# Attention of a two-layer mixer with keys instead of queries on the partitions

## The chip, the core and the metric

The kernel runs on one core of a Trainium2 chip, in one launch. The metric is the device time of a whole execution in microseconds (us), as the median of several runs. PE is TensorE, DVE is VectorE, ACT is ScalarE, POOL is GpSimd and SP is SyncE.

## What is computed

Two layers act on a sequence of 512 positions of width 1024. Each layer normalizes, projects, runs four branches (short convolution, sparse attention, retention, pooled means), gates and merges them, and ends with a gated feed-forward part. The change touches the attention branch:

```python
s_c = einsum('bsgjd,bngd->bgjsn', q, k_c)            # 31 compressed keys
p_c = masked_softmax(s_c, mask_c) * mask_c
o_cmp = einsum('bgjsn,bngd->bsgjd', p_c, v_c)
...
# o_slc, o_win: causal softmax attention over all 512 keys
# (all 8 blocks are among the 16 chosen, the window is 512 wide)
o = g[..., 0:1] * o_cmp + g[..., 1:2] * o_slc + g[..., 2:3] * o_win
```

There are eight heads in two key groups of four, each 64 wide. The selected and the window branch have keys and values of their own, so there are 16 causal attentions of 512 by 512 a layer.

## The kernel before

All activations lie transposed, features on partitions and 512 positions along the free axis. Every dense projection is a tile of 128 features by 512 positions in one of two PSUM banks (`acc`). It is made in full precision from F32R products: for each chunk of 128 inputs, `product` (L1107 to L1109) issues weights' high part by activations' high part, high by low, and low by high. Below, a product is one such 128x512 matmul.

Weights stream in groups of eight chunks through a ring of three buffers. SP loads `w_raw`, ACT rounds it to `w_hi` (L431), POOL subtracts to `w_lo` in two halves (L415), and each starts on a buffer when PE has left it. DVE empties each tile (`take`, L650) and PE may use a bank again when that is done. A layer runs stage A (12 groups: keys, values, queries, gates), stage B (32 groups: inputs of the other branches), the merge, the output projection and the feed-forward part.

The small work of the branches is spread over stage B. A group's four quarters, six products each, are the **slots**, 128 in all. The table `SIDE` names for each slot the steps that stand behind its products, and all engines walk through the same table in the same order, so the order on every queue is fixed by hand. Engines meet at counting semaphores.

Attention takes slots 4 to 71. Queries are on the partitions. A unit is one branch, one block of 128 queries and one head; two heads, one of each key group, go together, on the upper and lower 64 rows of PE's array. `scores` (L1266) makes a row of up to 512 scores. DVE adds the causal mask and takes the row's maximum in one instruction (L823). ACT takes the exponential with the maximum as its bias and the row's sum on the side (L513), and scales by gate over sum (L519). PE turns the probabilities in 128x128 pieces (`turn`, L1274), DVE copies them out of PSUM (L842), and `values` (L1292) multiplies. The compressed scores are eight small matmuls for each block of queries (L1253), masked, scaled and turned likewise; their values join the same output bank.

Retention follows with four heads (`RET_SLOT`). `ret_scores` (L1316) is multiplied by a decay table on DVE (L872) and feeds `ret_values` (L1326). The table comes by a DMA on ACT's queue (L498). The rotation of retention's queries and keys needs their halves exchanged, by two DMAs on ACT's queue (`rotate_partners`, L459, L460), and three DVE operations (L690 to L694).

## Time and profile before

| | before |
|---|---|
| median of 3 runs | 2152.51 us (2152.16 to 2152.82) |
| profiled execution | 2152.31 us |
| its span | 2150.5 us |
| PE, DVE, ACT, POOL busy | 97%, 57%, 31%, 43% |

Busy time of PE counts overlapping records once, and the records' ends are modelled; the distance between two starts tells what a matmul costs. Positions are us from the span's start. Line numbers are those of the kernel before.

### The profile page before, as it was taken

How to read it: one execution, taken by the hardware profiler on the slowest of the kernel's cores; microseconds unless marked ns; L12 is line 12 of the kernel's file. 1: busy time of each engine (PE TensorE's matmuls, PEld its weight loads, DVE VectorE, ACT ScalarE, POOL GpSimd, SP SyncE). 2: the span in 40 equal slices, each digit the busy share in tenths (PEclk: the TensorE clock that was granted, in tenths of full speed). 3: DMA queues.
4: the chain of work that ended last, by engine and by line, in shares of the span. 5: the costliest groups of instructions: out<-in, count | busy, mean ns of one | idle time of the engine just before them, and what ended most of it. 6: DMA issues, size and time to landing. Idle time of an engine off the chain costs nothing.

```text
span 2150.5 us, 32302 instructions
## 1 busy us (share of the span) xinstructions
PE 2086.4 (97%) x9834; PEld 1643.1 (76%) x9834; DVE 1227.3 (57%) x1856; ACT 659.8 (31%) x961; POOL 920.8 (43%) x676
## 2 busy tenths in 40 slices
PE   7999989999999999999999999999999999999997
PEld 5766667788888788888877666668888887888885
DVE  8656766622235888872157568565223278888513
ACT  3244423333332222222223445223233322222222
POOL 3422223444444555545534222234444454555552
PEclk9999999999999999999999999999999999999998
DMA  5311122222222222223232111222322232222332
GB/s 188 103 55 50 50 64 89 85 93 96 98 98 98 88 98 98 98 90 109 98 122 93 50 40 50 77 86 88 102 94 96 98 98 89 97 98 98 101 107 98
DMA packets 57131, 194.90 MB, mean 91 GB/s; under 512 B 6864, under 2 KB 7248, under 8 KB 56912
## 3 DMA queue, kind: packets, MB, share of 16 engines
q1 hardware_dynamic: 52272, 186.14, 26.1%
q10 hardware_dynamic: 4768, 7.61, 1.4%
q8 instruction: 50, 0.82, 0.2%
q14 instruction: 41, 0.34, 0.1%
HBM read 186.64 MB, written 2.10 MB: 88 GB/s over the span
## 4 chain that ended last, share of the span: by engine, by line
PE 91%; DVE 6%; issue 2%; ACT 0%; DMA 0%; DVEq 0%; ACTq 0%; SPq 0%
PE acc L1107 27%; PE acc L1109 27%; PE acc L1108 27%; PE o L1292 2%; PE s L1266 2%; PE t L1274 2%; PE o L1326 1%; PE s L1253 1%; PE s L1316 1%; PE s L1183 0%; PE t L1303 0%; DVE ssq L639 0%; DVE xg_lo L618 0%; PE s L1342 0%; DVE y_lo L900 0%
## 5 line engine op out<-in xcount | busy, mean ns | idle before, releaser
L415 POOL TENSOR_TENSOR w_lo<-w_raw,w_hi 128x512 fp32r<-128x512 f32 x672 | 920.6, 1390 | 1202.1 <-ACT w_hi L431 1190.4
L1107 PE MATMUL acc<-xg_hi,w_hi 128*128 128x512 f32 x1904 | 780.1, 410 | 18.4 <-DVE xg_lo L618 11.5
L1109 PE MATMUL acc<-xg_hi,w_lo 128*128 128x512 f32 x1904 | 748.9, 393 | 0.0
L1108 PE MATMUL acc<-xg_lo,w_hi 128*128 128x512 f32 x1904 | 748.0, 393 | 0.0
L431 ACT ACTIVATE w_hi<-w_raw 128x1024 fp32r<-128x1024 f32 x336 | 355.1, 1057 | 902.0 <-PE acc L1109 837.8
L1107 PEld LDWEIGHTS acc<-xg_hi,w_hi 128*128 128x128 f32 x1904 | 360.8, 190 | 127.3 <-issue 38.8
L1109 PEld LDWEIGHTS acc<-xg_hi,w_lo 128*128 128x128 f32 x1904 | 361.0, 190 | 77.8
L1108 PEld LDWEIGHTS acc<-xg_lo,w_hi 128*128 128x128 f32 x1904 | 361.7, 190 | 76.4 <-issue 6.9
L987 DVE TENSOR_TENSOR work<-acc,rstd 128x512 f32<-128x512 f32 x64 | 44.1, 690 | 256.1 <-PE acc L1109 256.1
L1107 PE MATMUL acc<-act_hi,w_hi 128*128 128x512 f32 x352 | 136.9, 389 | 0.0
L1108 PE MATMUL acc<-act_lo,w_hi 128*128 128x512 f32 x352 | 136.9, 389 | 0.0
L1109 PE MATMUL acc<-act_hi,w_lo 128*128 128x512 f32 x352 | 136.9, 389 | 0.0
L1081 DVE SCALAR_TENSOR_TENSOR x<-acc,x 128x512 f32 x16 | 11.1, 693 | 177.5 <-PE acc L1109 177.5
L993 DVE SCALAR_TENSOR_TENSOR work<-work,acc 128x512 f32<-128x512 f32 x64 | 44.0, 687 | 103.1 <-PE acc L1109 103.1
L1107 PE MATMUL acc<-y_hi,w_hi 128*128 128x512 f32 x256 | 99.6, 389 | 0.0
L1108 PE MATMUL acc<-y_lo,w_hi 128*128 128x512 f32 x256 | 99.6, 389 | 0.0
L1109 PE MATMUL acc<-y_hi,w_lo 128*128 128x512 f32 x256 | 99.6, 389 | 0.0
L566 ACT ACTIVATE work<-work 128x512 f32<-128x512 f32 x44 | 27.8, 632 | 186.4 <-DVE work L1036 186.4
L1108 PEld LDWEIGHTS acc<-act_lo,w_hi 128*128 128x128 f32 x352 | 66.1, 188 | 13.8
L1107 PEld LDWEIGHTS acc<-act_hi,w_hi 128*128 128x128 f32 x352 | 66.1, 188 | 13.7
L1109 PEld LDWEIGHTS acc<-act_hi,w_lo 128*128 128x128 f32 x352 | 66.1, 188 | 13.7
L842 DVE COPY pT<-t 128x128 f32<-128x128 f32 (+3 forms) x128 | 56.8, 486 | 28.3 <-PE t L1274 27.4
(190 smaller groups left out, 2231.1 us busy)
## 6 DMA issues: line engine op xcount, KB each, us to landing
w_raw<-weights_dram SPq DMA_DIRECT2D x339, 512.0 KB, 3.3
x<-xT_dram SPq DMA_DIRECT2D x8, 256.0 KB, 6.1
rot<-rq ACTq DMA_DIRECT2D x16, 128.0 KB
rot<-rk ACTq DMA_DIRECT2D x16, 128.0 KB
dec<-decay_dram ACTq DMA_DIRECT2D x8, 256.0 KB, 3.6
out_dram<-x SPq DMA_DIRECT2D x8, 256.0 KB, 2.2
con<-consts_dram SPq DMA_DIRECT2D x1, 1598.0 KB, 10.8
w1k<-w_dram SPq DMA_DIRECT2D x2, 512.0 KB, 9.3
```

Of the source, the lines that this page charges most:

```text
L415: nc.gpsimd.tensor_tensor(w_lo[:, k, part], w_raw[:, k, part], w_hi[:, k, part].bitcast(F32), ALU.subtract).then_inc(lo_ready, 1)
L431: nc.scalar.activation(w_hi[:, slot, :], w_raw[:, slot, :], ACT.Copy).then_inc(hi_ready, 1)
L566: nc.scalar.activation(work[:, 2, :], work[:, 1, :], ACT.Tanh, scale=0.5).then_inc(silu_ready, 1)
L842: t_end(ve.tensor_copy(pT[:, u % 2, 0:w], t_of(e)[:, 0:w]), e)
L987: ve.tensor_tensor(work[:, n, :], acc[n % 2][:, :], rstd[:, :], ALU.mult).then_inc(acc_free, 1)
L993: ve.scalar_tensor_tensor(out=work[:, n, :], in0=work[:, n, :], scalar=1.0, in1=acc[n % 2][:, :], op0=ALU.add, op1=ALU.mult).then_inc(acc_ ...
L1107: mm(tile, w_h, right_hi, start=first, stop=False)
L1108: mm(tile, w_h, right_lo, start=False, stop=False)
L1109: return mm(tile, w_l, right_hi, start=False, stop=last)
L1266: mm(b[:, 0:w], qT[r, h % 4, qi * P:(qi + 1) * P], kT[r, br, 0:w], start=True, stop=True).then_inc(s_done, 1)
L1274: ins = nc.tensor.transpose(b[:, k * P:(k + 1) * P], pr_of(u)[:, k * P:(k + 1) * P], ident)
L1292: ins = mm(o_bank[qi % 2][d, j * P:(j + 1) * P], v[:, d], p[:, half, :], start=(br == 0 and k == 0), stop=(br == 1 and k == qi + 1))
```

## The change

Keys now lie on the partitions and the probabilities come out in the orientation that the values need, so nothing is turned. The maximum runs along partitions then, so it is found ahead.

- **Maxima.** In slots 4 to 43, 40 quarters, PE makes all scores once more with queries on partitions, from F32R copies, into two banks a visit (`max`, 32 visits; `cmp_max`, 4). DVE writes minus the maximum into `table`. In slot 45 PE turns the table into rows, `shift`.
- **Pairs.** From slot 49 on, eight pairs (a branch and one head of each key group) take two slots each. A visit `scores` makes two blocks of keys for both heads: a first matmul with a repeated column of the identity adds the shift, a second the scores. ACT takes exponentials straight from PSUM, POOL zeroes what lies in the future (`affine_select`), and `values` multiplies. DVE adds the four blocks (`sums`), and PE sums that over partitions (`sum`) with selectors, 16 equal rows a head.
- **Factors.** `share`: DVE takes the reciprocal of a branch's sums and multiplies by the gates; ACT's queue spreads each row over 64 partitions with eight DMAs; `merge` multiplies and adds. There are three, for compressed, selected and window branch.
- **Homes and banks.** The two branches' outputs have buffers of their own. The scores ring has four banks in place of two and two for turns. Head 0 of retention moves from slot 68 to 71, and its decay table to the group of slot 68.

```diff
+PAIRS = 2 * BC
+VISITS = ((0, 3), (1, 2))
+MAX_SLOT = 4
+MAXES = [("max", _br, _qi, _j) for _br in range(2) for _qi in range(QT) for _j in range(BC)]
+for _n, _e in enumerate(MAXES):
+    SIDE[MAX_SLOT + 5 * _n // 4].append(_e)
+for _qi in range(QT):
+    SIDE[MAX_SLOT + 10 * _qi + 9].append(("cmp_max", _qi))
+TURN_SLOT = MAX_SLOT + 41
+SIDE[TURN_SLOT].append(("max_turn",))
+SIDE[TURN_SLOT + 1].append(("cmp_scores",))
+SIDE[TURN_SLOT + 3] += [("cmp_sum",), ("cmp_values",)]
+SIDE[TURN_SLOT + 4].append(("share", 0))
+PAIR_SLOT = [TURN_SLOT + 4 + 2 * _p for _p in range(PAIRS)]
+for _p in range(PAIRS):
+    SIDE[PAIR_SLOT[_p]].append(("scores", _p, 0))
+    SIDE[PAIR_SLOT[_p] + 1].append(("scores", _p, 1))
+for _p in range(PAIRS):
+    SIDE[PAIR_SLOT[_p] + 1].append(("values", _p, 0))
+    SIDE[PAIR_SLOT[_p] + 2] += [("values", _p, 1), ("sums", _p)]
+    SIDE[PAIR_SLOT[_p] + 3].append(("sum", _p))
+for _b in range(3):
+    if _b:
+        SIDE[PAIR_SLOT[BC * _b - 1] + 4].append(("share", _b))
+    for _j in range(BC):
+        _s = PAIR_SLOT[BC * _b - 1] + 8 if _b else TURN_SLOT + 9
+        SIDE[_s + _j // 2].append(("merge", _b, _j))
+ATTN_END = PAIR_SLOT[-1] + 4
...
+            def causal_part(L, p, v):
+                pool.wait_ge(con_ready, 16)
+                for k in VISITS[v]:
+                    s_freed(pool, L, ("scores", p, v, k, KV_GROUPS - 1))
+                    alone(pool)
+                    own = p_of(p, k)[:, :, 0:P]
+                    ins = nc.gpsimd.affine_select(own, own, [[0, KV_GROUPS], [1, P]], ALU.is_ge, zero, base=0, channel_multiplier=-1)
+                ins.then_inc(p_ready, 1)
...
+                        if B_TILES[b - 1] == ("rq", 1):
+                            act.wait_ge(v_made, v_count(L, ("merge", 2, 1)))
                         rotate_partners(L, B_TILES[b - 1])
...
+                        if b == max(14 + 4 * h, 17 + h):
+                            if h < 2:
+                                act.wait_ge(pv_done, pv_count(L, ("sum", PAIRS - 1)))
+                            else:
+                                s_freed(act, L, ("ret_scores", h - 2, QT - 1))
                             act.dma_start(dec[:, h % 2, :], decay[h, :, :]).then_inc(dec_ready[h % 2], 16)
...
+                            elif e[0] == "cmp_values":
+                                for j in range(BC):
+                                    act.wait_ge(s_done, s_use(L, (*e, j)))
+                                    free_s(nc.scalar.activation(o_all[:, j, :], s_of((*e, j))[:, :], ACT.Copy), (*e, j))
+                            elif e[0] == "scores":
+                                p, v = e[1], e[2]
+                                if v == 0:
+                                    if p < 2:
+                                        act.wait_ge(pv_done, pv_count(L, ("cmp_sum",)))
+                                        act.wait_ge(s_done, s_use(L, ("cmp_values", BC - 1)))
+                                    else:
+                                        act.wait_ge(pv_done, pv_count(L, ("sum", p - 2)))
+                                if p:
+                                    act.wait_ge(v_made, v_count(L, ("sums", p - 1)))
+                                    act.wait_ge(pv_done, pv_count(L, ("values", p - 1, 1 if v else 0)))
+                                for k in VISITS[v]:
+                                    for g in range(KV_GROUPS):
+                                        use = (*e, k, g)
+                                        act.wait_ge(s_done, s_use(L, use))
+                                        free_s(nc.scalar.activation(p_of(p, k)[:, g, 0:S - k * P], s_of(use)[:, 0:S - k * P], ACT.Exp,
+                                                                    scale=DH ** -0.5), use)
...
+                            elif e[0] == "share":
+                                b_ = e[1]
                                 act.wait_ge(v_made, v_count(L, e))
-                                nc.scalar.activation(cmp_p[:, :, :], cmp_p[:, :, :], ACT.Exp,
-                                                     scale=DH ** -0.5).then_inc(a_made, 1)
-                            elif e[0] == "scores":
-                                u = e[1]
-                                act.wait_ge(s_free, 1 + s_use(L, e) + 1)
-                                nc.scalar.activation(pr_of(u), pr_of(u), ACT.Exp, bias=nmax[:, u % 2:u % 2 + 1], scale=-1.0,
-                                                     accum_out=den[:, u % 4:u % 4 + 1]).then_inc(a_made, 1)
-                            elif e[0] == "scale":
-
-                                act.wait_ge(v_made, v_count(L, e))
-                                for u in (e[1], e[1] + 1):
-                                    nc.scalar.activation(pr_of(u), pr_of(u), ACT.Copy, scale=scl[:, u % 4:u % 4 + 1]).then_inc(a_made, 1)
+                                for j in range(BC):
+                                    if b_:
+                                        act.wait_ge(v_made, v_count(L, ("merge", b_ - 1, j)))
+                                    for g in range(KV_GROUPS):
+                                        row = recip[64 * g + 16 * j + b_:64 * g + 16 * j + b_ + 1, :]
+                                        act.dma_start(shared[64 * g:64 * g + 64, j, :],
+                                                      bass.AP(row.tensor, row.offset, [list(row.ap[0]), [0, DH], [1, S]])).then_inc(share_here[j], 16)
...
+                def max_(e):
+                    br, qi, j = e[1:]
+                    w = (qi + 1) * P
+                    s_wait((*e, KV_GROUPS - 1))
+                    for g in range(KV_GROUPS):
+                        s = s_of((*e, g))[:, 0:w]
+                        at_ = 64 * g + BC * br + j
+                        alone(dve)
+                        s_end(ve.tensor_tensor_reduce(s, s, C("causal", S)[:, S - w:S], -1.0, 3e38, ALU.add, ALU.min,
+                                                      table[:, qi, at_:at_ + 1]), (*e, g))
...
+                def sums(e):
+                    p = e[1]
+                    dve.wait_ge(p_ready, p_ready_count(L, ("scores", p, 1)))
+                    dve.wait_ge(pv_done, pv_count(L, ("values", p, 0)))
+                    for k in (1, 2, 3):
+                        all_ = p_of(p, 0)[:, :, k * P:S]
+                        ins = ve.tensor_tensor(all_, all_, p_of(p, k), ALU.add)
+                        if k < 3:
+                            then(ins)
+                    v_end(ins, e)
+                def share(e):
+                    b = e[1]
+                    dve.wait_ge(pv_done, pv_count(L, ("sum", BC * b - 1) if b else ("cmp_sum",)))
+                    ve.reciprocal(recip[:, :], o_of(("den", b))[:, :]).then_inc(o_free[1], 1)
+                    o_freed(dve, L, ("den", b))
+                    v_end(ve.tensor_tensor(recip[:, :], recip[:, :], gates[:, :], ALU.mult), e)
...
+                    o_freed(dve, L, ("pair", BC * (b - 1) + j))
+                    part = part_of(b, j)
+                    then(ve.tensor_tensor(part, part, shared[:, j, :], ALU.mult))
+                    v_end(ve.tensor_tensor(all_, all_, part, ALU.add), e, wait=(b == 2))
+                    if b == 2:
+                        split_y(1, j, all_)
...
+                def max_(e):
+                    br, qi, j = e[1:]
+                    w = (qi + 1) * P
+                    pe.wait_ge(a_made, a_count(L, f"q_r{j}"))
+                    banks = s_begin(*[(*e, g) for g in range(KV_GROUPS)])
+                    last_wait()
+                    for g, b in enumerate(banks):
+                        r = rows_of(g)
+                        ins = mm(b[:, 0:w], q_r[r, j, qi * P:(qi + 1) * P], k_r[r, br, 0:w], start=True, stop=True)
+                        ins.then_inc(s_done, 1)
...
+                    banks = s_begin(*uses)
+                    pe.wait_ge(const_made, L + 1)
                     last_wait()
-                    mm(b[:, 0:w], qT[r, h % 4, qi * P:(qi + 1) * P], kT[r, br, 0:w], start=True, stop=True).then_inc(s_done, 1)
-
-                def turn(e):
-                    u = e[1]
-                    pe.wait_ge(a_made, a_count(L, ("scale", u)))
-                    b = t_begin(e)
+                    at_ = BC * br + j
+                    four = [(k, rows_of(g), g, banks[uses.index((*e, k, g))]) for k in VISITS[v] for g in range(KV_GROUPS)]
+                    for k, r, g, b in four:
+                        mm(b[:, 0:S - k * P], spread(ident_r[r, 64 * g + at_:], [[0, P]]), shift[r, k * P:S], start=True, stop=False)
+                    for k, r, g, b in four:
+                        mm(b[:, 0:S - k * P], kT[r, br, k * P:(k + 1) * P], qT[r, j, k * P:S],
+                           start=False, stop=True).then_inc(s_done, 1)
...
+                    own = ones_at[:, 16 - 16 * (j % 2):48 - 16 * (j % 2)]
+                    for g in range(KV_GROUPS):
+                        c = 64 * g + 32 * (j // 2)
+                        ins = mm(den[c:c + 32, :], own, p_of(p, 0)[:, g, :], start=(j % 2 == 0), stop=(j % 2 == 1), skip_group_check=True)
+                    ins.then_inc(pv_done, 1)
```

The queue of ACT in the pairs. Before, for two scores steps of 256 keys (`pr_odd`, `pr` are score rows):

```order
L431 ACTIVATE w_hi<-w_raw 128x1024 [waits raw_ready0]
L512 REGISTER_ALU
L513 ACTIVATE pr,small<-pr,small 128x256 [waits s_free]
L512 REGISTER_ALU
L513 ACTIVATE pr,small<-pr,small 128x256 [waits s_free]
L517 REGISTER_ALU
L519 ACTIVATE pr<-pr,small 128x256 [waits v_made]
```

Of the change, where the pairs open (`o_all` takes the compressed values, `shared` the spread factors, `p_` the probabilities of key blocks):

```order
L646 ACTIVATE o_all<-s 128x512 [waits s_done]
L676 REGISTER_ALU
L682 DMA shared<-recip 64x1x512 [waits v_made]
L682 DMA shared<-recip 64x1x512 x7
L651 ISA
L661 REGISTER_ALU [waits s_done,pv_done]
L662 ACTIVATE p_zero_104<-s 128x512 [waits s_done]
L661 REGISTER_ALU
L662 ACTIVATE p_zero_104<-s 128x512 [waits s_done]
```

Eight DMAs now stand between the emptying of the compressed values and the first exponentials.

ACT's queue before the decay table `dec` of retention head 0, before:

```order
L519 ACTIVATE pr_odd<-pr_odd,small 128x512 [waits v_made]
L519 ACTIVATE pr_odd<-pr_odd,small 128x512
L429 REGISTER_ALU
L431 ACTIVATE w_hi<-w_raw 128x1024 [waits raw_ready1,halves]
L498 DMA dec<-decay_dram 128x512
```

Of the change:

```order
L682 DMA shared<-recip 64x1x512
L530 REGISTER_ALU
L532 ACTIVATE w_hi<-w_raw 128x1024 [waits raw_ready1,halves]
L616 REGISTER_ALU
L556 REGISTER_ALU [waits v_made]
L558 REGISTER_ALU [waits acc_free]
L560 DMA rot<-rq 64x512 [waits v_made]
L561 DMA rot<-rq 64x512
L623 REGISTER_ALU
L626 DMA dec<-decay_dram 128x512 [waits pv_done]
```

The rotary DMAs with their wait, and the last of the share DMAs, now stand ahead of it.

DVE at the first retention scores, before:

```order
L650 TENSOR_TENSOR rq<-acc,rstd 128x512 [waits halves]
L651 REGISTER_ALU
L655 REGISTER_ALU [waits acc_free]
L868 ISA [waits s_done]
L872 TENSOR_TENSOR pr<-s,dec 128x512 [waits dec_ready0]
L665 REGISTER_ALU
L841 REGISTER_ALU [waits t_done]
L842 COPY pT<-t 128x512 [waits pv_done]
```

Of the change (`o_early`, `o_third` hold window outputs):

```order
L1032 TENSOR_TENSOR o_all<-o_all,o_early 128x512 [waits chain]
...
L1072 CAST y_hi_56<-o_all 128x512 [waits v_made]
...
L1073 TENSOR_TENSOR y_lo_60<-o_all,y_hi_56 128x512 [waits chain]
...
L1045 TENSOR_TENSOR pr<-s,dec 128x512 [waits dec_ready0]
...
L1031 TENSOR_TENSOR o_third<-o_third,shared 128x512 [waits o_free0]
...
L1032 TENSOR_TENSOR o_all<-o_all,o_third 128x512 [waits chain]
...
L1072 CAST y_hi_56<-o_all 128x512 [waits v_made]
...
L1073 TENSOR_TENSOR y_lo_60<-o_all,y_hi_56 128x512 [waits chain]
...
L1045 TENSOR_TENSOR pr<-s,dec 128x384 [waits s_done]
```

Merges now stand before and between the two retention scores.

## Rows read from the trace of the kernel before

**Rows 1.** The page, parts 1, 4 and 5.

```profile
PE 2086.4 (97%) x9834; PEld 1643.1 (76%) x9834; DVE 1227.3 (57%) x1856; ACT 659.8 (31%) x961; POOL 920.8 (43%) x676
...
PE 91%; DVE 6%; issue 2%; ACT 0%; DMA 0%; DVEq 0%; ACTq 0%; SPq 0%
...
L415 POOL TENSOR_TENSOR w_lo<-w_raw,w_hi 128x512 fp32r<-128x512 f32 x672 | 920.6, 1390 | 1202.1 <-ACT w_hi L431 1190.4
...
L431 ACT ACTIVATE w_hi<-w_raw 128x1024 fp32r<-128x1024 f32 x336 | 355.1, 1057 | 902.0 <-PE acc L1109 837.8
```

**Rows 2.** The timeline of PE: start and duration in us, line, operation, tiles.

```profile
1000.19 0.39 PE L1107 MATMUL acc<-act_hi,w_hi 128*128 128x512 f32 x1
...
1005.63 0.39 PE L1107 MATMUL acc<-act_hi,w_hi 128*128 128x512 f32 x1
```

**Rows 3.** Busy time by stretch of line L1107 alone, second layer.

```profile
1154.40:1354.00 199.60, 61.24 (x136) 25.78 (x135) 0.98 0.17 55
```

**Rows 4.** The timeline of PE around a scores and a values step.

```profile
201.29 0.40 PE L1109 MATMUL acc<-xg_hi,w_lo 128*128 128x512 f32 x1
201.62 0.92 PE L1266 MATMUL s<-kT,qT 64*128 64x384 f32 x4
...
202.80 0.39 PE L1108 MATMUL acc<-xg_lo,w_hi 128*128 128x512 f32 x1
...
203.73 0.40 PE L1109 MATMUL acc<-xg_hi,w_lo 128*128 128x512 f32 x1
204.06 0.88 PE L1292 MATMUL o<-pT,v_nat 128*64 128x128 f32 x12
...
205.23 0.87 PE L1274 MATMUL t<-con,pr 128*128 128x128 f32 x6
...
206.17 0.39 PE L1108 MATMUL acc<-xg_lo,w_hi 128*128 128x512 f32 x1
```

**Rows 5.** The timeline of PE around a compressed-scores step.

```profile
229.56 0.40 PE L1109 MATMUL acc<-xg_hi,w_lo 128*128 128x512 f32 x1
229.89 1.87 PE L1253 MATMUL s<-kc,qT 64*128 64x31 f32 x13
...
233.99 0.40 PE L1108 MATMUL acc<-xg_lo,w_hi 128*128 128x512 f32 x1
```

**Rows 6.** The timeline of ACT, two neighbours of 512 columns.

```profile
1357.70 0.60 ACT L527 ACTIVATE pT<-o 128x512 f32<-128x512 f32 x1 [4.57 <-issue]
1358.19 0.59 ACT L528 ACTIVATE pT<-o 128x512 f32<-128x512 f32 x1
```

**Rows 7.** Groups of DVE instructions by form: busy us, mean ns, idle before.

```profile
L1091 DVE RECIPROCAL rstd<-rstd 128x512 f32<-128x512 f32 x1 | 3.4, 3353 | 2.7 <-ACT rstd L585 2.7
...
L937 DVE TENSOR_TENSOR y_lo<-sc,y_hi 128x512 fp32r<-128x512 f32 x8 | 9.5, 1193 | 0.1
...
L933 DVE TENSOR_TENSOR sc<-sc 128x512 f32<-128x512 f32 x8 | 5.5, 693 | 0.3
```

**Rows 8.** The timeline of ACT, DMA issues of the rotary partners.

```profile
49.62 0.63 ACTq L453 DMA_DIRECT2D rot<-kT  x1
50.28 0.63 ACTq L452 DMA_DIRECT2D rot<-kT  x1
```

**Rows 9.** Line L459: duration ns min/median/max of the issues.

```profile
L459 ACTq DMA_DIRECT2D rot<-rk x8: 468/468/482, 109.7 to 1427.3; - x8
```

**Rows 10.** The tile of the decay table.

```profile
DMA to landing us min/median/max: 2.6/3.6/4.8
```

**Rows 11.** PE before and at retention head 1, then that stretch's busy time.

```profile
1368.51 0.40 PE L1109 MATMUL acc<-xg_hi,w_lo 128*128 128x512 f32 x1
1372.39 2.07 PE L1316 MATMUL s<-rq,rk 128*128 128x512 f32 x2 [3.49 <-DVE rk L694]
...
1371.60:1378.30 6.70, 5.91 (x10) 3.47 (x11) 3.29 (x6) 0.00 (x0) 0.00 (x0) 0.50 0.23 78
```

**Rows 12.** PE's waits: us in total, times, longest us.

```profile
PE s L1316 <- DVE rk L694: 14.7, 6, 3.5
```

630 lines of the change are left out of this document (364 added, 266 removed).

## The prediction

> **What bounds the kernel now.** I read the page first, then the PE timeline in steady state and around the side steps, then the forms of DVE and ACT work, then the waits. TensorE is busy 97% of the span and holds 91% of the chain that ended last [rows 1]. A busy record says little here, because the records overlap: two records of the same line, 24 products apart, start 5.44 us apart, 0.2267 us per product [rows 2]. The program's 7920 products (3 for each of 2640 chunks) at that pitch are 1795 us of the 2150.5, so the rest of the span is side steps, waits and a slow clock. The kernel is bound by TensorE's queue: each side step is paid in full, and another engine costs something where PE waits for it.
>
> The changed stretch is slots 4 to 71 of stage B. In the second layer it runs from 1154.4 to 1354.0, 199.6 us, with 136 products of each of three lines [rows 3]: 408 products, 92.5 us. The other 107.1 us hold head 0 of the retention (2560 columns of full-array f32 at four passes, 2560/512 x 4 x 0.2267 = 4.5 us), its turn (about 0.5) and attention: **102 us a layer**, its waits included.
>
> **Unit prices on PE.** The scores step at 201.62 stands between products at 201.29 and 202.80 [rows 4]: 1.51 us, less two pitches, is 1.06. It holds a pair of 384-column f32 matmuls on the two row halves. One of them at four passes is 384/512 x 4 x 0.2267 = 0.68, so the second is free and entering and leaving the half-array costs 0.4. The values step at 204.06, from 203.73 to 206.17, costs 2.44 - 0.45 = 1.99: three pairs of 128 columns on column halves (0.68), the compressed pair, six turns at 0.11, and about 0.3 of switching. A compressed-scores step, between products at 229.56 and 233.99, costs 3.98 with a 512-column scores pair of 1.3 in it: 2.7 for matmuls of 31 columns [rows 5].
>
> **The change on PE, per layer.** F32R passes are 0.2267 per 512 columns, f32 four times that; each step pays 0.4 for switching, a step behind another about 0.2.
> - Maxima: 32 F32R pairs of 128 to 512 columns. The pairs cost 0.13 to 0.23 (short ones bounded by weight loads), 5.3 together, with 32 x 0.4: 18.
> - Compressed maxima, 4 x 0.9: 3.6. Mask turn, table turn and gate matmul: 1.8.
> - Scores, 16 visits: main products 8 x 1280 columns x 4 passes = 18.1, shift products 8 x 0.57 = 4.5, switching 6.4: 29.
> - Values: 18.1 + 16 x 0.2 = 21.3. Sums: 8 x (0.91 + 0.2) = 8.9.
> - Compressed scores (16 matmuls on 8 tiles), their sum and values: all tiles together, in rounds of 512/512 x 4 x 0.2267 = 0.9, two rounds, one and one with their switching, 2.3 + 1.2 + 1.3 = 4.8. Two tiles at a time, which is all that the row shows [rows 4], 7.7 + 1.2 + 4.0 = 12.9. I take 4.8, since there the second tile costs nothing visible, and keep 12.9 for the range.
>
> Sum: 87.4, plus 0.7 in stage A for eight small value products instead of two. That is 102 - 88 = **14 us a layer gained**, mostly from 160 probability turns, the compressed-scores steps and 32 f32 scores that become F32R.
>
> **The change in waits, per layer.** Three places queue long work ahead of what PE needs.
>
> *Opening of the pairs (slots 48 to 50).* Let T be the end of the compressed sum on PE. ACT empties four banks first; ACTIVATEs of 512 columns start 0.49 apart [rows 6], so scores (0,0) starts near T+3.2 instead of T+2.6: 0.6 of wait. DVE takes a reciprocal of 512 columns, 3.35 us, and a product of 0.7 [rows 7], done at T+4.3. ACT then issues eight DMAs. Two neighbouring issues are 0.66 apart and each holds the ACT queue for 0.63 [rows 8]; eight take 5.3 us, to T+9.6. Only behind them stand the exponentials of (0,0), 1.4 us. PE has finished scores (0,0) and slot 50's products at T+6.5 and needs their banks: it waits until T+11, **4.5 us**. The shortest issue that the trace shows is 0.47 [rows 9], which would make 3.8 of the 5.3.
>
> *Middle (slot 59).* The same eight DMAs stand before the exponentials of (5,1). Counted from the first finished pair of scores (4,1) at X: exponentials end X+1.4, POOL's selects X+2.1 (256 elements, taken at half of the 1.39 of a 512-element w_lo half [rows 1]; 0.1 to 1.4), the three adds X+4.2, reciprocal and product X+8.5, DMAs X+13.9, w_hi 1.06 [rows 1] and one more issue X+15.4, exponentials X+16.8. PE arrives at X+14: **2.8 us**.
>
> *End (slots 66 to 73).* Before, head 0 found its decay table long loaded. Now its ACT queue reads: eight share DMAs, w_hi, a wait for merge (2,1), two rotary DMAs, then the decay DMA. DVE comes to the sums late, since the last two merges of the first branch and a mean stand before it: 1.6 us for PE, and 0.8 before the reciprocal. With T now the end of the last sum: reciprocal and product T+5.1, the last mean part and a take (about 3.8) T+8.9, merge (2,0) with four operations T+11.6, two operations of merge (2,1) while POOL makes w_lo. Such SBUF-to-SBUF operations range from 0.69 to 1.2 [rows 7]; with 1.2 each T+14.2. Rotary DMAs T+15.5, the decay landing 3.6 later [rows 10] T+19.1, DVE's product T+19.9. PE stands at its first retention value from T+9.7: **10.2 us**. Then merges (2,2) and (2,3), eight operations of 0.69, precede DVE's second retention score: another **4.2 us**.
>
> The table turn in slot 45 waits for DVE's last maxima (two of 0.77 a step, with a convolution among them): 1.3. I add 1.0 for the other 13 visits, whose exponentials (1.4) are covered by 1.4 of products and 1.3 of values. New waits: 0.6 + 4.5 + 2.8 + 1.6 + 10.2 + 4.2 + 1.3 + 1.0 = **26 us a layer**.
>
> **Clock.** Before 1372.39 PE waited 3.49 us, and from 1371.6 to 1378.3 its granted clock was 0.50, the 1.2 GHz level [rows 11]. At half clock 6.7 us of work take what 3.4 would. Three long waits should bring this about up to four times a layer; two dips at the old compressed-scores steps may go. I take **+4**, range 0 to 8.
>
> Net per layer: -14 + 26 + 4 = +16, **+32 us** for two. The profiled execution took 2152.3 around a span of 2150.5, and the median of the runs is 2152.5, so either base gives **2184 us**.
>
> **A rule beside the row.** The scores step [rows 4] shows two tiles at a time and nothing about eight. The Trainium skill (TensorEngine Tiling (Array Packing), Key Properties) says that tiles work independently and may load and multiply in parallel. By that rule the compressed steps cost 4.8; by the pairing alone, 12.9, and the total would be 2200. No row here has more than two tiles at work.
>
> **Rivals.**
> 1. *Faster.* PE's saving is real and the waits shrink: ACT's issues are short, merges run uncontended, exponentials slip into the gaps. Only the decay chain stays, about 5 a layer: 2 x (-14 + 5) = -18, 2134. For it: before, PE lost only 14.7 us to its largest group of waits [rows 12], so its queue is well fed. Against it: the order of the ACT queue and 0.66 per issue. It decides if new waits and clock stay below 14 a layer.
> 2. *DVE bounds the pairs.* The adds of probabilities and merges read two SBUF tensors while POOL works more. If all run at 1.7 times, as y_lo's 1193 against 693 [rows 7], two slots hold 3.6 of sums, 5.3 of convolution, 2.9 of merges and 0.4 of takes, 12.2 us against PE's 10; over five pairs 11 us a layer: 2206. The Trainium skill (GPSIMD Engine Reference, Specifications) names this contention for DVE instructions with two SBUF inputs, and the spread in rows 7 agrees. Against it: POOL is busy only part of a group, and not every pair has convolution and merges.
> 3. *Tiles go two at a time*, for the want of more than two in any row: 2184 + 2 x 8.1 = 2200.
>
> **How the numbers follow.** Forecast 0.50, range of its own 2160 to 2208 (issues 0.47 or 0.66, contention, clock 0 to 8). Rival 1: 0.22. Rival 2: 0.18. Rival 3: 0.10. The 80% range reaches down to rival 1's 2134, since below the forecast it holds most of the chance, and to 2212, above rival 2. About 0.2% (4.3 us) is what a measurement of this kernel tells from no change; only rival 1's weak end lands there. Faster 0.20, same 0.05, slower 0.75.
>
> **What would show it.** In the changed profile PE waits of about 4.5 us at the second scores visit, released by ACT's exponentials; about 10 us at the first retention value, released by DVE's product with the decay table, and 4 at the next; a granted clock of 0.5 just after. Right on PE: max steps of about 0.55, no L1274-like turns. I am wrong if the exponentials start before the share DMAs end, if the retention values start on time, or if the stretch from the first maxima to the first retention score, waits left out, is not some 14 us a layer shorter.

## The result and the profile after

The changed kernel takes **2246.89 us** (median of 4 runs, 2244.48 to 2252.45), the kernel before on the same chip 2152.66: a ratio of 1.0438, 95% interval 1.0424 to 1.0453. The forecast was 2184, at most 2212. The direction is right; of 94 us of loss it had 32.

The page of the changed kernel, its parts 1, 3, 4 and 5, beside [rows 1]:

```profile
PE 2070.0 (92%) x9334; PEld 1601.1 (71%) x9334; DVE 1226.3 (55%) x1682; ACT 587.2 (26%) x739; POOL 953.6 (43%) x744
...
q10 hardware_dynamic: 8608, 13.90, 5.4%
...
PE 82%; DVE 9%; ACTq 5%; issue 3%; ACT 1%; DMA 1%; DVEq 0%; SPq 0%
PE acc L1280 25%; PE acc L1282 25%; PE acc L1281 25%; ACTq L682 4%; PE s L1516 1%; PE o L1531 1%; PE s L1438 1%; DVE recip L1015 1%; PE o L1569 1%; DVE y_lo L1073 1%; PE s L1514 1%; PE s L1559 1%; DMA dec<-decay_dram 1%; DVE p_zero L1006 0%; PE o L1546 0%
```

TensorE has less work and is idle more. New in the chain is ACT's DMA queue with 5%, nearly all of it line 682, the share DMAs. PE's waits (us in total, times, longest), whose largest group was 14.7 before [rows 12]:

```profile
PE o L1569 <- DVE pr L1045: 48.7, 8, 22.0
PE s L1514 <- ACT p_two L662: 30.1, 2, 16.6
PE s L1514 <- ACT p_three L662: 27.9, 2, 14.2
PE s L1559 <- DVE rk L853: 15.0, 6, 3.3
...
PE s L1461 <- DVE table L989: 1.5, 2, 0.8
```

These are the three places of the forecast: the opening (14.2, forecast 4.5), the middle (16.6, forecast 2.8) and the end (22.0, forecast 10.2). ACT's timeline at the opening shows why, beside [rows 8]:

```profile
189.46 2.06 ACT L646 ACTIVATE o_all<-s 128x512 f32<-128x512 f32 x4 [1.55 <-PE s L1499]
192.52 14.94 ACTq L682 DMA_DIRECT2D shared<-recip  x8
207.71 1.08 ACT L662 ACTIVATE p_zero<-s 128x512 f32<-128x512 f32 x2 [16.18 <-issue]
```

Eight issues hold ACT for 14.94 us, not for 5.3. The tile of the spread factors gives one issue (ns, minimum, median, maximum) and its landing:

```profile
L682 ACTq DMA_DIRECT2D shared<-recip x48: 476/1868/4254, 192.5 to 1426.5; - x48
...
DMA to landing us min/median/max: 6.2/7.9/10.1
```

At the end the slow transfers are paid for more than once, first on ACT's timeline:

```profile
310.91 15.03 ACTq L682 DMA_DIRECT2D shared<-recip  x8
...
326.34 1.41 ACTq L560 DMA_DIRECT2D rot<-rq  x1
327.77 2.68 ACTq L561 DMA_DIRECT2D rot<-rq  x1
330.56 0.91 ACTq L626 DMA_DIRECT2D dec<-decay_dram  x1
```

and then on DVE's, where the first merge waits for a landing and the decay product for the table:

```profile
320.28 0.69 DVE L1031 TENSOR_TENSOR o_early<-o_early,shared 128x512 f32<-128x512 f32 x1 [6.93 <-DMA shared<-recip]
...
324.25 0.69 DVE L1031 TENSOR_TENSOR o_early<-o_early,shared 128x512 f32<-128x512 f32 x1 [1.36 <-DMA shared<-recip]
...
336.20 0.69 DVE L1045 TENSOR_TENSOR pr<-s,dec 128x512 f32<-128x512 f32 x1 [9.34 <-DMA dec<-decay_dram]
...
343.07 0.56 DVE L1045 TENSOR_TENSOR pr<-s,dec 128x384 f32<-128x384 f32 x1
```

These operations of DVE themselves run at 0.69, uncontended. Of all share products (`o_all`, `o_slc` and the like from `shared`) the median is 0.69 and the longest 0.99.

PE's own prices are as forecast. Its timeline around a maxima step of 256 columns, and around the compressed scores with their 8 shift and 8 score matmuls, each of which leaves two records:

```profile
115.39 0.39 PE L1282 MATMUL acc<-xg_hi,w_lo 128*128 128x512 f32 x1
115.71 0.39 PE L1438 MATMUL s<-k_r,q_r 64*128 64x256 f32 x2
...
116.36 0.39 PE L1281 MATMUL acc<-xg_lo,w_hi 128*128 128x512 f32 x1
...
182.13 0.40 PE L1282 MATMUL acc<-xg_hi,w_lo 128*128 128x512 f32 x1
182.46 1.09 PE L1473 MATMUL s<-shift,con 64*32 64x512 f32 x16
183.34 1.06 PE L1477 MATMUL s<-qT,kc 64*32 64x512 f32 x16
...
184.67 0.39 PE L1281 MATMUL acc<-xg_lo,w_hi 128*128 128x512 f32 x1
```

Less two pitches [rows 2], the maxima step costs 116.36 - 115.39 - 0.45 = 0.52 (over the four widths 0.47 to 0.64, forecast 0.55), and the compressed scores 184.67 - 182.13 - 0.45 = 2.09 (forecast 2.3).

### The profile page after: what moved, and what is told of

It is laid out like the page before. It is cut to its first block, busy times and chain, and to the rows that moved or that the text cites. A ratio compares the mean times of both kernels' runs of the same rounds, so it can differ in the third digit from the quotient of the medians.

```text
span 2242.7 us, 30172 instructions
## 1 busy us (share of the span) xinstructions
PE 2070.0 (92%) x9334; PEld 1601.1 (71%) x9334; DVE 1226.3 (55%) x1682; ACT 587.2 (26%) x739; POOL 953.6 (43%) x744
## 4 chain that ended last, share of the span: by engine, by line
PE 82%; DVE 9%; ACTq 5%; issue 3%; ACT 1%; DMA 1%; DVEq 0%; SPq 0%
PE acc L1280 25%; PE acc L1282 25%; PE acc L1281 25%; ACTq L682 4%; PE s L1516 1%; PE o L1531 1%; PE s L1438 1%; DVE recip L1015 1%; PE o L1569 1%; DVE y_lo L1073 1%; PE s L1514 1%; PE s L1559 1%; DMA dec<-decay_dram 1%; DVE p_zero L1006 0%; PE o L1546 0%
## 5 line engine op out<-in xcount | busy, mean ns | idle before, releaser
L1006 DVE TENSOR_TENSOR p_zero<-p_zero,p_one 128x768 f32<-128x768 f32 x16 | 15.3, 958 | 129.6 <-PE o L1531 92.1
L970 DVE CUSTOM_DVE_ANT_0 s<-s,con 128x128 f32<-128x128 f32 (+3 forms) x128 | 60.6, 516 | 42.1 <-PE s L1438 35.2
L1281 PEld LDWEIGHTS acc<-act_lo,w_hi 128*128 128x128 f32 x352 | 66.1, 188 | 13.6
```

The lines of the kernel that those rows point to most:

```text
L970: s_end(ve.tensor_tensor_reduce(s, s, C("causal", S)[:, S - w:S], -1.0, 3e38, ALU.add, ALU.min, table[:, qi, at_:at_ + 1]), (*e, g))
L1281: mm(tile, w_h, right_lo, start=False, stop=False)
```

## The experiments

Theory A: the share DMAs are slow, and they stand before what PE needs. Its rivals put the loss on their number, on the price of an issue as such, or on what remains of the change without them. To compare kernels I read, in the first layer, the starts of the first products of slots 4, 71 and 80 and of the merge stage (J) on PE's timeline; the table holds the distances in us. The border at 71 cuts differently before and after: of retention's head 0 some 4.2 us stood ahead of 71 before and now stand behind it, and the last values step of the attention, some 1.5 us, stood behind it before (both are estimates from PE's timeline, 283.6 to 296.6). Each time is the median of its runs; the kernel before stood between 2152.7 and 2154.4 in the six series.

| kernel | time | 4 to 71 | 71 to 80 | 80 to J |
|---|---|---|---|---|
| before | 2152.7 | 196.0 | 17.0 | 97.1 |
| after | 2246.9 | 212.2 | 43.8 | 100.8 |
| e1_rows | 2181.4 | 192.1 | 31.8 | 100.8 |
| e3_none | 2154.4 | 178.2 | 30.4 | 103.5 |
| e5_paced | 2195.2 | 181.0 | 47.9 | 102.3 |
| e6_pe | 2169.9 | 184.1 | 30.7 | 104.3 |
| e9_pe_36 | 2168.9 | 183.7 | 32.5 | 100.0 |
| e13_late | 2156.5 | 183.2 | 24.4 | 103.6 |
| e14_late_u | 2150.1 | 182.7 | 19.7 | 106.1 |
| e17_ports | 2193.2 | 199.0 | 33.8 | 100.0 |
| e18_all | 2153.8 | 177.2 | 28.3 | 104.8 |

### What makes the transfers slow

**e1_rows**

```diff
-bass.AP(row.tensor, row.offset, [list(row.ap[0]), [0, DH], [1, S]])
+recip[64 * g:64 * g + 64, :]
```

> The same 48 transfers of 64 x 512 at the same places of ACT's queue, but each reads 64 rows of the factors instead of one row 64 times (the spreading is left out, so the branches are weighted by the wrong rows). Theory A, the one source row makes a transfer slow and the full queue holds up the issue: an issue falls from 1.87 us in the mean of its kind to 0.5 to 0.7, eight take about 5 us instead of 15.0, a landing falls from 7.9 to 2 to 3 us, TensorE's waits of 16.6 and 14.2 us at the scores go to about 3 and 5, the DMA share in these stretches from 0.7 to 0.8 to under 0.4, and the time to the forecast's 2175 to 2195. Theory B, eight transfers of 128 KB in a row are what costs, whatever they read: an issue stays at 1.5 to 2 us and the time within 10 us of 2247.

2181.41 us, ratio 1.0128 (1.0109 to 1.0146). ACT's timeline and the landing:

```profile
192.10 5.09 ACTq L682 DMA_DIRECT2D shared<-recip  x8
197.43 1.08 ACT L662 ACTIVATE p_zero<-s 128x512 f32<-128x512 f32 x2 [6.33 <-issue]
...
DMA to landing us min/median/max: 2.2/2.3/2.5
```

Theory A: it is the source, not the count. PE's three waits in this run:

```profile
PE o L1569 <- DVE pr L1045: 27.5, 9, 9.9
...
PE s L1514 <- ACT p_three L662: 8.5, 2, 4.3
PE s L1514 <- ACT p_two L662: 7.3, 2, 4.5
```

This run also is nearly the forecast, since its issues have the price that the forecast gave them: longest waits of 4.3, 4.5 and 9.9 against 4.5, 2.8 and 10.2, and 2181 against 2184. It leaves out the spreading itself, so it says what such transfers cost and is no kernel to use.

**e4_dram**: `row = decay[0, ...]` in place of `row = recip[...]`, again repeated 64 times; the branches are weighted by wrong values.

> The same 48 transfers with the same pattern, one row of 2 KB repeated 64 times, but the row is read from DRAM (from the decay table) instead of from one SBUF partition; the values are wrong ones. Theory A1, it is the one SBUF partition that is slow to read 64 times: an issue at 0.5 to 0.7 us, a landing at 2 to 3.5 us, the time 2175 to 2195. Theory A2, a repeated row is slow wherever it lies (the pattern, or one address hit 64 times): issue 1.5 to 2 us, landing 6 us or more, the time within 15 us of 2247.

2181.21 us. The same pattern from DRAM costs what 64 rows cost, so a repeated row isn't slow as such:

```profile
L682 ACTq DMA_DIRECT2D shared<-decay_dram x48: 472/617/717, 192.5 to 1361.3; - x48
...
DMA to landing us min/median/max: 2.8/3.3/4.4
```

**e2_one**

```diff
-act.dma_start(shared[64 * g:64 * g + 64, j, :],
-              bass.AP(row.tensor, row.offset, [list(row.ap[0]), [0, DH], [1, S]]))
+pair = [[64 * row.ap[0][0], KV_GROUPS], [0, DH], [1, S]]
+act.dma_start(shared[:, j, :], bass.AP(row.tensor, row.offset, pair))
```

> One transfer to 128 partitions for each block of four heads in place of two to 64: 24 issues instead of 48, the same bytes read from the same rows. Theory A, the queue is full of packets and lets the next issue in as they drain: an issue takes about twice as long (3.5 to 4 us), the four about 15 us as the eight did, and the time stays within 10 us of 2247. Theory C, each issue has a price of its own that its pattern with a repeated row sets: an issue stays near 1.9 us, the four take 7.5, and the time falls by about 2 x 3 x 5 = 30 us.

2230.47 us, between the two. Four issues take 9.52 us (0.60, 0.54, 3.14, 5.15), with 256 KB each: neither half of 15 nor all of it. The first two are short, the next are held. I take this as a queue that lets a few transfers in and then holds the issue until one has drained, which no run tests by itself; theory C, one price for each issue, fits neither these four nor the 0.5 and 0.6 to 0.7 at the head of each eight. The edit changed more than the count, as the end of this section shows.

**e16_four**: the gates' selector repeats each gate in five neighbouring rows (three small copies more), and a transfer reads four of them, `[list(row.ap[0]), [0, DH // 4], [1, S]]`.

> The changed kernel with one edit: the factors of a branch stand in five rows of the tile instead of one (the gates' selector repeats each gate five times), and a transfer reads four of them 16 times each, instead of one row 64 times. The result is the same. If the limit is how fast one SBUF partition is read (theory A1), four partitions are read at once: an issue at 0.6 to 0.8 us, a landing at 2.3 to 4 us, the time 2178 to 2192, as with 64 rows. If the four rows are read one after the other, each by all 16 engines, nothing is won: 2235 to 2247, issue still over 1.5 us.

2242.71 us: 4 us won, and the first range missed. **e17_ports**

```diff
-spread(ident, [[12, KV_GROUPS], [3, BC], [1, 16]])
+spread(ident, [[3, KV_GROUPS * BC], [0, 4], [1, 4]])
-[list(row.ap[0]), [0, DH], [1, S]]
+[[4 * row.ap[0][0], 4], [0, DH // 4], [1, S]]
```

> The changed kernel with one edit: the factors of a branch stand in four rows of the tile that lie four partitions apart (the gates' selector repeats its rows with period four), and a transfer reads these four 16 times each, in place of one row 64 times. The result is the same. Theory A2, SBUF is read by transfers through ports that each serve groups of four partitions, so that four neighbouring rows (the run before) were no better than one, but four rows with steps of four are read at once: an issue at 0.6 to 0.8 us, a landing at 2.3 to 4 us, the time 2178 to 2192, as with 64 rows. Theory A3, it is the number of times that a row is repeated, or the pattern with a repeat in it, that makes the packets slow: an issue at 1.3 to 1.9 us and the time 2235 to 2247, as with four neighbouring rows. The Trainium skill (SBUF — State Buffer, the section on the DMA port swizzle) gives the mapping that A2 rests on.

2193.15 us, ratio 1.0184 (1.0169 to 1.02), 1 us above A2's range and far below A3's. The traces of these two runs have no landings. ACT's queue in the two, all eight issues of a branch, first e16_four in its three branches:

```profile
193.79 17.96 ACTq L682 DMA_DIRECT2D shared<-recip  x8
...
264.71 13.03 ACTq L682 DMA_DIRECT2D shared<-recip  x8
...
316.93 12.03 ACTq L682 DMA_DIRECT2D shared<-recip  x8
```

then e17_ports in its first:

```profile
192.01 7.18 ACTq L682 DMA_DIRECT2D shared<-recip  x8
```

Both read four rows 16 times each. Four rows with steps of four are quick; four neighbours aren't, and they are slowest in the first branch, whose rows 0 to 3 lie in one group of four partitions, and less slow in the second and third, whose rows 5 to 8 and 10 to 13 lie in two. With one row the three branches hold ACT alike, for 14.9, 15.2 and 15.0. So what counts here is how many groups of four partitions the source has. The Trainium skill (SBUF — State Buffer, Door 1: The DMA port swizzle) says just this: neighbouring partitions in fours share a port, and it gives one port 27.2 GB/s. By that figure 128 KB take 4.8 us (an estimate), and eight, in turn on the ports of the two partition halves, 19.3 (an estimate too). The trace agrees: the burst's 1.05 MB pass between 193.6 and 213.0, in 19.4 us.

A second thing changed unseen with the source pattern, the number of DMA engines at work. ACT's DMA queue in the first burst (packets, MB, busy share of the 16 engines), for the changed kernel (193.6 to 213.0), e1_rows (193.2 to 198.6), e16_four (195.0 to 217.5), e17_ports (193.2 to 204.1) and e2_one (193.6 to 215.1):

```profile
q10 hardware_dynamic: 640, 1.05, 79.9%
...
q10 hardware_dynamic: 640, 1.05, 85.0%
...
q10 hardware_dynamic: 544, 1.05, 21.8%
...
q10 hardware_dynamic: 544, 1.05, 25.5%
...
q10 hardware_dynamic: 520, 1.05, 12.8%
```

Each burst has 512 packets of 2 KB; the rest are of 4 bytes, 16 for each of the eight transfers in the first two kernels, 4 in e16_four and e17_ports, and 2 for each of the four in e2_one. With the busy shares this says that a transfer whose source pattern begins with a count of 4 ran on 4 of the 16 engines, and one that begins with 2 on 2. Those of 64 rows, and of one row 64 times, ran on all 16. So e17_ports against e16_four, 10.7 against 22.5 us for the same bytes on 4 engines each, is a clean test of the rows' place. What was left between e17_ports and e1_rows, 0.81 against 0.62 an issue, goes with 4 engines against 16 (10.7 against 5.4 us for the burst). And e2_one, at 21.5 us, was held by 2 engines as well as by its rows, so it doesn't tell the two apart. Why four neighbours on 4 engines take longer than one row on 16 (22.5 against 19.4) stays open.

### How much is place, and how much the rest of the change

**e3_none**: no DMA; `merge` multiplies by `recip[:, :]`, so the spreading is left out.

> No transfer at all: the merges multiply by the 128 rows of factors as they stand (the spreading is left out, the output is wrongly weighted), and ACT's queue has neither the issues nor their waits. This is the floor of what the rest of the change can give. Theory A and C alike: TensorE waits nowhere at the scores for more than 1 us, the last wait (for the decay table and the rotary merges) is left at 5 to 10 us a layer, and the time is 2152.7 - 2 x 14 (the matmul work saved) + 2 x 8 = 2125 to 2150. A rival that the transfers only uncover (the visits of 512 columns themselves, the exponentials or DVE's sums bound the pairs): the waits stay near 10 us a layer at the scores and the time is over 2170.

2154.41 us, ratio 1.0 (0.9989 to 1.001), above the expected range. The transfers thus cost 2242.7 - 2154.1 = 88.6 us of the two spans; fast ones (e1_rows) would cost 27. And the rest of the change gains nothing. By the table the stretch to slot 71 is 17.8 us shorter; less the 4.2 of retention that moved and plus the 1.5 of the last values step, the attention is about 15 us shorter, where 14 was forecast. About 11 us are lost between 71 and 80 and 6.4 behind (4.4 in the second layer); before slot 4 the first layer loses 2.8 and the second nothing. PE's timeline, where DVE is late with the decay product:

```profile
290.52 2.04 PE L1558 MATMUL o<-pr,rv 128*128 128x512 f32 x2 [7.60 <-DVE pr L1034]
```

**e5_paced**: the slow DMAs, for one block of heads in each slot, behind the exponentials.

```diff
+SIDE[(PAIR_SLOT[BC * _b - 1] + 4 if _b else TURN_SLOT + 4) + (_j // 2 if _b == 2 else _j)].append(("issue", _b, _j))
```

> The slow transfers are kept, with one SBUF row as the source, but they are issued two at a time in four slots of their own, behind each slot's exponentials (for the third branch four and four, in two slots). Theory A, the queue takes two or three such transfers at once and then holds the issuing engine for as long as one takes to drain: two in a slot of about 5 us are issued in 0.5 and 0.6 us, TensorE's waits at the scores fall from 14.2 and 16.6 us to under 2 each, the end of the attention keeps 17 to 22 us, and the time is 2247 - 2 x 28 = 2185 to 2200. Theory C, each issue costs ACT 1.9 us wherever it stands: two cost 3.8 in a slot, the scores wait 1 to 3 us in each of eight slots, and the time is 2205 to 2235.

2195.21 us. No wait over 0.8 us is left at the scores; slots 72 and 73 take 18.7 and 12.1 longer than their six products. So of 94 us, 52 came from eight in a row at the wrong place. The queue shows here too: the second pair of issues took 0.47 and 3.80, where 0.5 and 0.6 were expected.

**e7_dec**: the decay table's load stands ahead of the rotary pair.

> The slow transfers stay; only the load of the decay table is issued ahead of the pair of rotary transfers, and of the wait for the third branch's second merge, instead of behind them. If the last wait (22.0 us at the retention's first value product) is the decay table's, which follows all of these on ACT's queue, it falls by 3 to 8 us a layer and the time to 2231 to 2241. If it is the landing of the eight transfers and the merges behind them, ahead of the decay product on DVE, it stays over 20 us and the time at 2243 to 2250.

2243.84 us, in the rival's range, though the longest wait, 19.0 in place of 22.0, is in the first's. The table's place is worth 3 us a layer there, of which the attention, 215.0 in place of 212.2 by the table's measure, gave as much back in the first layer; why is not shown. The other 19 us are not the table's place.

**e6_pe**: the factors, rounded to F32R, are spread by PE. There are four F32R matrices of ones by blocks, written by DVE once a layer, 12 matmuls a layer, and one instruction of DVE that keeps one row of 16 for each head.

```diff
+mm(b[:, :], rows_r[:, j, :], recip_r[:, :], start=True, stop=True).then_inc(s_done, 1)
-ve.tensor_tensor(part, part, shared[:, j, :], ALU.mult)
+ve.tensor_tensor(part, part, s_of(use)[:, :], ALU.mult)
```

> No transfer: TensorE spreads the factors, with one matmul of 128 x 128 x 512 in F32R for each of the 12 merges of a layer into a score bank, from which the merge reads them; the factors are rounded to F32R and masked to their branch's row in the same instruction of DVE that multiplies by the gates. If the transfers and their place are the whole loss, this stands at the run without them plus 2 x 12 x 0.23 to 0.35 us: 2154.4 + 5.5 to 8.4 = 2160 to 2163, with 2156 to 2170 as its range. If a merge that holds a score bank makes the next scores wait (DVE's list of 0.7 us steps stands ahead of it), 1 to 3 us come at each of the four slots in which scores follow merges, and the time is 2165 to 2180.

2169.91 us, where the two ranges overlap, so that the time doesn't decide. The slots speak for the rival: 184.1 against 178.2 us up to slot 71, and slot 55, behind the merges of the compressed branch, takes 5.46 more than its products, in place of 3.08. **e8_both**, with e7_dec's edit as well:

> The spreading on TensorE together with the decay table's earlier load. In the run without transfers the first decay product waited 2.99 us on DVE for the table; with that gone DVE's own list bounds it: 3 us a layer less than with the spreading on TensorE alone, 2151 to 2158. If the load collides with something or DVE is late by as much anyway, no less than 2158.

2171.56 us, a miss; the second case, DVE late by as much anyway, holds. The decay product came earlier, but DVE took the same time for its list: the loss moved from slot 72 (10.7 to 7.7) to slots 73 and 74 (3.6 to 6.0, 0.8 to 2.7).

### DVE's list behind the pairs

Four kernels give the attention more room before the retention, two with PE's spreading and two with the paced transfers (the third branch's now in four slots too), all with e7_dec's edit. The maxima take 36 slots (with `_n` alone, 32):

```diff
-SIDE[MAX_SLOT + 5 * _n // 4].append(_e)
+SIDE[MAX_SLOT + 9 * _n // 8].append(_e)
```

> Spreading on TensorE, the decay table's load ahead of the rotary ones, and the maxima packed into 36 slots instead of 40, so that everything behind them up to the third branch's merges stands four slots (some 6 us of products) earlier, while the retention keeps its slots. If the end wait (7.7 us at the first value product and 4 us at the second) is DVE's list of the third branch's reciprocal and merges being late for the decay products, it goes nearly whole: 8 to 11 us a layer less than with both edits alone, 2149 to 2156. If packing the maxima makes DVE (busy 37.9 of 52 us in these slots before) the bound there, it gives 3 to 8 us a layer back and the time stays over 2158.

> The same with the maxima in 32 slots, one in each, and all behind them eight slots earlier. DVE's 37.9 us of work in 26 slots of 2.0 us come into 20.8 slots of 2.1, 0.87 of the time, if TensorE isn't held: the same time as with 36 slots within 3 us if the end was already clear, up to 8 us less if it wasn't; over 2160 if the two banks of a maximum come free too late for the next (TensorE then waits 0.3 us or more at each of the 32 maxima).

> The slow transfers, exact in F32, issued two at a time in four slots, with the maxima in 36 slots and the decay table's load ahead of the rotary ones. The paced run lost 18.7 and 12.1 us at slots 72 and 73 (before: 0.3 and 0.1), behind the third branch's transfers. Four slots more are worth 6 us of products, and the third branch's transfers can now be paced as well: the two slots lose 10 to 20 us instead of 31, and the time is 2195 - 2 x (11 to 21) = 2153 to 2173.

> The same with the maxima in 32 slots. The third branch's transfers end some 12 us of products ahead of the retention's first value product, so that no wait of more than 3 us stands at slots 72 and 73 if the place was the whole rest: 2195 - 2 x 27 = 2135 to 2150, the first of these kernels to beat the kernel before (2152.8) by what the saved matmul work is worth. If the transfers slow something else (the weights' loads, DVE's merges), it stays over 2155.

2168.86, 2169.82, 2169.11 and 2170.93 us. Of the ranges of improvement only e11_paced_36's held, and e10_pe_32 was within 3 us of e9_pe_36. With either place and either way of spreading, the time is 2169 to 2171. In e9_pe_36 PE now waits at slot 71, for DVE to empty a projection bank. DVE's timeline there has no gap over 0.3 us from 264.57 to 299.6, the reciprocal and the decay product among it:

```profile
272.21 3.36 DVE L1014 RECIPROCAL recip<-o 128x512 f32<-128x512 f32 x1
275.60 1.79 DVE L1016 SCALAR_TENSOR_TENSOR recip_r<-recip,small,gates 128x512 fp32r<-128x512 f32 x1
...
284.01 0.69 DVE L1032 TENSOR_TENSOR o_early<-o_early,s 128x512 f32<-128x512 f32 x1 [0.21 <-DVE sc L1122]
...
291.39 0.69 DVE L816 TENSOR_TENSOR rq<-acc,rstd 128x512 f32<-128x512 f32 x1
...
298.92 0.69 DVE L1046 TENSOR_TENSOR pr<-s,dec 128x512 f32<-128x512 f32 x1 [0.22 <-DVE y_lo L1074]
```

PE's side steps end with the pairs, and its products then go by at 1.36 us a slot: slots 61 to 70 take it 19.3 us. DVE has the means of the pooling tiles, the third reciprocal, the merges and their splits to do for them, and needs 35.

Two kernels shorten the list. **e13_late** puts the last two merges behind the decay products, and all splits in slots 84 to 87; **e14_late_u** also projects three pooling tiles earlier (`POOL0 = [28, 10, 11, 12]`, `SC0 = [4, 7, 13, 29]`).

> As with 36 slots of maxima and the spreading on TensorE, but the third branch's last two merges (four operations of DVE each with their splits) stand behind the retention's decay products, in slots 74 and 75, and all four splits into high and low halves in slots 84 to 87. In the run with 36 slots DVE worked without a gap from 261 to 299.5 us and its first decay product came at 298.9, behind these. If DVE's own list is what bounds the end, 7.0 us of it (292.3 to 298.9, and two splits of 1.2 before that) leave it and TensorE's loss at slots 71 to 73 falls from 17.8 to 9 to 12 us: the time is 2169 - 2 x (6 to 9) = 2151 to 2157. If it was the decay table or a score bank, no change: 2165 or more.

> As e13, and three of the pooling tiles, whose running means cost DVE some 10 us, are projected three groups earlier, in the place of a convolution's tiles (about 5 us of DVE), so that DVE's list behind the pairs is some 5 us shorter. If DVE's list is the bound there: another 3 to 5 us a layer, 2143 to 2151, faster than the kernel before. If the means then hold up the pairs' sums (the denominators' matmuls wait for them): no gain, 2151 to 2160.

2156.51 us and **2150.14 us**, ratio 0.998 (0.997 to 0.999). Both are in their ranges: DVE's list was the bound. e14_late_u is 0.2% faster than the kernel before, and the fastest of all. The gain is small: 3.4 us, under the 4.3 that the prediction took as the least that a measurement tells from no change, though the interval lies below 1. PE still waits for DVE, now at slot 91, behind the splits in slots 84 to 87:

```profile
PE acc L1287 <- DVE rk L821: 5.2, 1, 5.2
```

> The same two edits of DVE's list, on the kernel with the slow transfers from one row, issued in pairs, exact in F32 and without the 5 us a layer that the spreading costs TensorE. In that kernel (36 slots) DVE waited 4.4 us for two landings of the third branch. With DVE's list shorter by 12 us a layer and the landings left: 2169.1 - 2 x (8 to 13) = 2143 to 2153. If the landings now bound the merges that the rotary transfers wait for, 2153 to 2162.

2163.15 us, a miss, 1 us above the rival's range: the landings of slow transfers (DVE waited 6.3 us for two) and the table behind them (9.2) now stand first. **e18_all** has e17's rows, e15's order, and the splits in slots 99 to 102.

> All that the runs have pointed to, and nothing left out of the computation: the rows of e17 as the source, two transfers to a slot, the decay table's load ahead of the rotary ones, maxima in 36 slots, the pooling tiles three groups earlier, the third branch's last two merges behind the decay products, and its splits in slots 99 to 102, where DVE was busy for 1.9 of 10 us. Against the fastest run so far (2150.1) it saves what the spreading on TensorE cost (some 6 to 7 us a layer at the pairs) and the wait of 5.35 us at slot 91 that the splits in slots 84 to 87 had made: 2150 - 2 x (6 + 5) = 2128, with 2124 to 2140. If the transfers are no faster than from one row, it stands at 2163 less the 5 us a layer: 2150 to 2158.

2153.84 us, ratio 0.9995 (0.9985 to 1.0004), a clear miss. The time lies in the second range, but not for its reason, since the transfers are quick (an issue 0.55 in the median). The attention is at its shortest (177.2), but slots 71 to 73 lose 13.6 us, with DVE again waiting 1.4 for a landing and 3.8 for the decay table, and slot 107 loses 4.2 behind the splits.

The 6.4 us that e3_none lost from slot 80 on in the first layer can be read from its trace. PE's waits there sum to 11.7 us against 8.6 before, and 10.2 us pass at a granted 0.50 with PE busy for 8.7, against 3.4 before, all busy. At the full level that work would take half, so the clock costs 4.4 against 1.7 (estimates from these figures). Both together are 5.8. That the order of DVE's list makes these waits was not tested.

## Why the prediction was wrong in size

- **The failed step** is the price of the share DMAs: "Two neighbouring issues are 0.66 apart and each holds the ACT queue for 0.63 [rows 8]; eight take 5.3 us, to T+9.6." The neighbours [rows 8] read eight partitions each. Those of the change read one 64 times: 1.87 an issue, 14.9 to 15.0 for eight. With the landings that follow from it, this is 2246.9 - 2181.4 = 65.5 us, all of the 62.9 by which the forecast was short. Where the issues have the forecast's price (e1_rows), it is right to 3 us.
- **Part of those 3 us is luck.** By e1_rows the middle wait was 1.7 us longer than forecast, and behind slot 80 3.7 us were lost in the first layer, for which the sum had no term. Against that the second wait at the end, forecast 4.2, was 2.6 at most (12.5 for all four waits of a layer, less 9.9), and the 1.6 before the last sum never came.
- The sum also had a merge start as soon as its issue was over. The landing, 7.9, wasn't in it, nor that the rotary and decay transfers wait in the same queue: 4.1 for two rotary issues instead of 1.3, 5.6 from the decay's issue to DVE's product instead of 3.6 [rows 10].
- I had kept both ends for the issue, 0.47 and 0.66, from rows of transfers with other sources. The range held no case in which the new pattern itself was slow. The range's top would have had to be near 2250 to hold that case.
- **PE's work** was right: about 15 us a layer less in e3_none where 14 was forecast, by a reading of the borders that is good to about 1 us, the maxima at their price, the compressed scores 2.09 where 2.3 was taken. All tiles work together, so rival 3 falls. The rule of the Trainium skill (TensorEngine Tiling (Array Packing), Key Properties) that tiles work independently agrees with these rows.
- **The places** were right, all three, and by e1_rows the opening and the first wait of the end to 0.3 us. The table turn waited 0.8, not 1.3.
- **Clock**, +4 a layer forecast, was right. The three long stretches at a granted 0.50 (the 1.2 GHz level), with PE's busy time first:

```profile
198.70:212.30 13.60, 3.11 (x14) 1.86 (x16) 0.00 (x0) 2.32 (x7) 0.76 (x2) 0.50 0.80 61
267.00:284.00 17.00, 3.27 (x14) 1.92 (x16) 2.53 (x5) 2.79 (x6) 3.29 (x4) 0.50 0.71 91
318.20:342.00 23.80, 4.87 (x9) 2.87 (x10) 10.39 (x17) 2.11 (x2) 4.96 (x4) 0.50 0.74 121
```

  PE worked 11.3 us of them, and would have needed half at the full level: 5.6 a layer (an estimate). Beside them two stretches of 3.4 us at 0.50 are left in this part of the first layer, where the kernel before had three, and PE worked 6.6 us of them instead of 10.2. The net is 5.6 + 3.3 - 5.1, about +4. In 43 of the 54.4 us of the long stretches PE stood idle, and there the slow level costs nothing.
- **Rival 2** (DVE) fell as it was put: the merges' operations ran at 0.69 in the median and 0.90 in the mean of their slowest group, not 1.2. As a count of work it was half right: behind the pairs, not in them, DVE's list was what kept the saved matmul work from showing. **Rival 1** wanted the waits to shrink: even with no transfer at all (e3_none) the time is 2154, not 2134.

## What to carry to other kernels

The price of a transfer here was that of its source, at the same size, destination and queue: a row from the trace is a price only for a transfer that reads as many partitions, as far apart, by a pattern with the same counts. Give a transfer that repeats SBUF rows a source that is spread over the partitions, and put it behind what its queue's engine owes to others. Work saved on the busiest engine shows only if the next one keeps up just behind it: count its list there, in the stretch in which the first has nothing but its own work left.

## What the runs showed of the hardware

- Reading one SBUF row 64 times (128 KB): issue 1.87 us, landing 7.9 (the changed kernel). From 64 rows 0.62 and 2.3 (e1_rows), from one DRAM row 0.62 and 3.3 (e4_dram). Four neighbouring rows (e16_four) hold ACT for 18.0 us in eight issues when they lie in one group of four partitions, and for 13.0 and 12.0 when they lie in two; four rows with steps of four (e17_ports) for 7.2.
- A source pattern that begins with a count of 4 or 2 kept 4 or 2 of the 16 DMA engines at work, one of 64 rows all of them: busy shares of 25.5% (e17_ports) and 12.8% (e2_one) against 85.0% (e1_rows).
- ACT's queue took two or three such transfers at once; the next issue then held the engine, up to 4.25 us.
- In the three long stretches around these bursts the 16 DMA engines were 0.71 to 0.80 busy at 61 to 121 GB/s. A rotary issue of 128 KB behind a burst took 2.68 us instead of 0.62.
- GpSimd's `affine_select` of 128x256 took 0.40 to 0.51 us in the mean of its groups, under the 0.70 that was taken.
